# Output gates of a gated linear attention made from a tanh, and two weight splits moved into the state chain

## The reference

```python
def gla_mixer(h, s0, w_in, w_gate, b_gate, norm_w, w_out):
    q, k, v, r, gl = jnp.split(h @ w_in, ...)
    ...
    o, s_new = gla_recurrence(q, k, v, log_a, s0)
    o = rms_norm(o, norm_w) * jax.nn.silu(r.reshape(N, T, H_C, DV_C).astype(jnp.float32))
    return o.reshape(N, T, H_C * DV_C).astype(h.dtype) @ w_out, (s_new,)
```

## Time and profile before

| | |
|---|---|
| median of 3 runs | 1903.7 us (1898.15 to 1910.28) |
| the profiled execution | 1904.86 us, of which its span is 1903.2 |
| PE busy | 1788.3 us (94%) |
| DVE busy | 889.6 us (47%) |
| ACT busy | 465.1 us (24%) |
| POOL busy | 78.5 us (4%) |
| mean granted TensorE clock | 0.94 |

### The profile page before, as it was taken

The page is one execution under the profiler, slowest core; times in us unless marked ns, Lnnn a source line. Parts: engine busy times, 40 slices in busy tenths (PEclk is TensorE's granted clock), DMA queues, the critical chain, the costliest instruction groups (busy, mean ns, idle before and its releaser), DMA issues.

```text
span 1903.2 us, 32761 instructions
## 1 busy us (share of the span) xinstructions
PE 1788.3 (94%) x14212; PEld 1630.2 (86%) x14212; DVE 889.6 (47%) x1650; ACT 465.1 (24%) x746; POOL 78.5 (4%) x146
## 2 busy tenths in 40 slices
PE   5979999999999899999999899878988999999998
PEld 3768888777768899999999897767878999999997
DVE  3534243344344653636353523376565745454442
ACT  1512221134463311111111324122322311111112
POOL 2000001500030000000000000000000000000000
PEclk7889999989999999999999999877779999999998
DMA  9657665410062222222223465122232222222211
GB/s 352 227 196 248 223 199 166 177 51 1 23 223 90 67 79 78 88 88 87 67 88 126 146 199 177 46 70 70 70 120 89 67 89 72 82 88 88 78 54 50
DMA packets 160179, 218.83 MB, mean 115 GB/s; under 512 B 7271, under 2 KB 131198, under 8 KB 159630
## 3 DMA queue, kind: packets, MB, share of 16 engines
q1 hardware_dynamic: 148814, 177.52, 28.4%
q0 software_dynamic: 11264, 39.86, 6.0%
HBM read 199.66 MB, written 21.76 MB: 116 GB/s over the span
## 4 chain that ended last, share of the span: by engine, by line
PE 89%; DVE 7%; ACT 1%; DMA 1%; issue 1%; SPq 0%; ACTq 0%; DVEq 0%
PE ps L1365 14%; PE ps L1363 14%; PE ps L1362 14%; PE ps L1041 4%; PE ps L1042 4%; PE ps L1043 4%; PE ps L918 3%; PE ps L1151 2%; PE ps L1328 2%; PE ps L1329 2%; PE ps L1331 2%; PE ps L1137 2%; PE ps L967 1%; PE ps L1166 1%; PE ps L1459 1%
## 5 line engine op out<-in xcount | busy, mean ns | idle before, releaser
L1362 PE MATMUL ps<-arena_r,wring_r 128*128 128x288 f32 x2048 | 570.1, 293 | 7.4 <-DVE hbuf_r L2131 7.4
L1365 PE MATMUL ps<-arena_r,wring_r 128*128 128x288 f32 x2048 | 439.6, 296 | 0.0
L1362 PEld LDWEIGHTS ps<-arena_r,wring_r 128*128 128x128 f32 x2048 | 386.0, 188 | 7.7 <-issue 7.7
L1365 PEld LDWEIGHTS ps<-arena_r,wring_r 128*128 128x128 f32 x2048 | 328.3, 188 | 0.0
L1363 PE MATMUL ps<-hbuf_r,wring_r 128*128 128x288 f32 x1024 | 286.1, 295 | 0.0
L1363 PE MATMUL ps<-arena_r,wring_r 128*128 128x288 f32 x1024 | 284.6, 294 | 0.0
L1833 ACT ACTIVATE wring_r<-wring 128x2048 fp32r<-128x2048 f32 x64 | 122.5, 1917 | 620.5 <-DMA wring<-in_mlp_w 620.5
L1363 PEld LDWEIGHTS ps<-hbuf_r,wring_r 128*128 128x128 f32 x1024 | 193.9, 189 | 0.0
L1363 PEld LDWEIGHTS ps<-arena_r,wring_r 128*128 128x128 f32 x1024 | 192.4, 188 | 0.0
L2469 DVE SCALAR_TENSOR_TENSOR xbuf<-ps,mod,xbuf 128x288 f32<-128x288 f32 (+1 forms) x128 | 56.1, 480 | 245.5 <-PE ps L1365 245.5
L1041 PE MATMUL ps<-wring_r,xbuf_r 128*128 128x512 f32 x360 | 149.9, 416 | 0.0
(11 more groups left out here) (378 smaller groups left out, 2627.2 us busy)
## 6 DMA issues: line engine op xcount, KB each, us to landing
wring<-in_mlp_w SPq DMA_DIRECT2D x64, 1024.0 KB, 5.2
arena<-in_ada_w SPq DMA_DIRECT2D x40, 1024.0 KB, 5.8
wring<-in_even_w_in SPq DMA_DIRECT2D x14, 1024.0 KB, 8.2
wring<-in_gla_w_in SPq DMA_DIRECT2D x12, 1024.0 KB, 5.6
wring<-in_ada_w SPq DMA_DIRECT2D x4, 2048.0 KB, 28.1
xbuf<-xspill SPq DMA_DIRECT2D x2, 2304.0 KB, 9.3
arena<-in_cache_cmp_kv POOLq DMA_DIRECT2D x16, 256.0 KB, 10.1
wring<-in_cache_diff_k POOLq DMA_DIRECT2D x16, 256.0 KB, 3.6
```

The lines of the kernel that those rows point to most:

```text
L1362: pe.matmul(bank, hi, x_hi[:, k, cols], start=k == 0, stop=False)
L1365: mm = pe.matmul(bank, lo, x_hi[:, k, cols], start=False, stop=k == KC - 1)
```

## The change

Four edits, all in layer 1's recurrence:

- ACT's exponential of -r becomes a tanh of r/2 (one instruction for one, same buffers, same waits).
- A gate becomes one DVE instruction, (tanh + 1) times r, in place of three.
- The factor 1/2 and the norm weight go elsewhere: the two columns of norm weight in `v2T` are halved once, before the recurrence, and `g_gated` multiplies output, halved weight and gate in one scalar_tensor_tensor, where it was a tensor_tensor.
- The low halves of `W_R[2]` and `W_R[3]` are no longer made after the last gate of heads 0 and 1 but inside the chain of heads 1 and 2, after its first two states.

```diff
--- before.py
+++ after.py
@@ -1937,7 +1937,7 @@
                 act.wait_ge(r_kept, i + 1)
                 if i >= 2:
                     act.wait_ge(r_ready, i - 1)
-                act.activation(er[i % 2], gr[:, i // 2, halves[i % 2]], ACT.Exp, scale=-1.0).then_inc(r_exp, 1)
+                act.activation(er[i % 2], gr[:, i // 2, halves[i % 2]], ACT.Tanh, scale=0.5).then_inc(r_exp, 1)
 
             def g_square(h):
 
@@ -2602,6 +2602,8 @@
                     dve.sem_inc(st_kept, 1)
                     if h == 0 and p < 2:
                         rest_unit(W_R[p], S_GIN + 8 + p)
+                    elif 1 <= h <= 2 and p == 0:
+                        rest_unit(W_R[h + 1], S_GIN + 9 + h)
                     if h + 1 < HC:
                         if p == 1:
                             g_offsets(h + 1)
@@ -2624,17 +2626,16 @@
 
                 c, cols = i // 2, halves[i % 2]
                 dve.wait_ge(r_exp, i + 1)
-                step(dve.tensor_scalar(er[i % 2], er[i % 2], 1.0, None, ALU.add))
-                step(dve.reciprocal(er[i % 2], er[i % 2]))
-                dve.scalar_tensor_tensor(out=gr[:, c, cols], in0=gr[:, c, cols], scalar=v2T[:, V2_GLAN + c % 2:V2_GLAN + c % 2 + 1],
-                                         in1=er[i % 2], op0=ALU.mult, op1=ALU.mult).then_inc(r_ready, 1)
+                dve.scalar_tensor_tensor(out=gr[:, c, cols], in0=er[i % 2], scalar=1.0, in1=gr[:, c, cols],
+                                         op0=ALU.add, op1=ALU.mult).then_inc(r_ready, 1)
 
             def g_gated(h):
 
                 dve.wait_ge(r_mm, 2 * KC)
                 dve.wait_ge(go_kept, h + 1)
                 for e in range(2):
-                    ins = dve.tensor_tensor(hT[:, 2 * h + e, :], go[:, e, h, :], gr[:, 2 * h + e, :], ALU.mult)
+                    ins = dve.scalar_tensor_tensor(out=hT[:, 2 * h + e, :], in0=go[:, e, h, :], scalar=v2T[:, V2_GLAN + e:V2_GLAN + e + 1],
+                                                   in1=gr[:, 2 * h + e, :], op0=ALU.mult, op1=ALU.mult)
                 return ins
 
             for u in range(len(gin)):
@@ -2654,6 +2655,7 @@
                 elif u == V_HALF + 2:
                     g_from_blocks(0)
             dve.wait_ge(ada_kept, 2 * ADA)
+            dve.tensor_scalar(v2T[:, V2_GLAN:V2_GLAN + 2], v2T[:, V2_GLAN:V2_GLAN + 2], 0.5, None, ALU.mult)
             step(dve.memset(gatt[:, :, :, :], 0.0))
             g_scores(0)
             g_sample_keys(0)
@@ -2679,8 +2681,6 @@
                     if h + 2 < HC:
                         for i in range(at + 3, last):
                             r_gate(i)
-                    if h < 2:
-                        rest_unit(W_R[h + 2], S_GIN + 10 + h)
             ins = g_gated(HC - 1)
             step(ins)
             head_rates(1)
```

## The result

| | before | changed |
|---|---|---|
| median of 16 runs each | 1905.14 us (1896.19 to 1912.58) | 1889.55 us (1882.84 to 1902.42) |
| ratio of the runs | | 0.9925 (95%: 0.9905 to 0.9944) |
| span of the profiled execution | 1903.2 us | 1881.7 us |
| PE's waits for L2596 | 18.8 us | 2.8 us |
| first L1476 of head 0's samples to first L1328 of the output projection ("the stretch") | 152.63 us | 135.27 us |

The changed kernel is faster by 0.75% (0.56 to 0.95%); 1886.6 us and a ratio of 0.9910 were forecast.

What follows compares the result with a forecast made beforehand. PE was taken to bound the kernel, waiting on DVE for the first state at the seams between heads. Terms 8.9 + 6.85 + 1.4 = 17.1 us took 1903.7 to 1886.6 us, range 1878 to 1893.5.

Steps and rivals of the forecast that it cites:

- What bounds it: Recurrence: PE, 89% of the chain, waits 18.8 us for L2596, one wait per seam, the third 0.3 us.
- First seam: Between heads 0 and 1: three shorter gates and the moved low half let L2596 start 8.9 us sooner.
- Second seam: Between heads 1 and 2: two shorter gates and the moved low half let L2596 start 6.85 us sooner.
- The moved low halves: Behind the first state steps of heads 1 and 2: cost nothing, 2.28 us each under 7.31 us of DVE idle time.
- rival 2: Heads 1 and 2: no cover for the moved low halves, gain only 12.1 us, time 1891.6 us; chance 0.09.
- After the last head: End of head 3: shorter gates free DVE before PE starts, so PE leads; 1.4 us gained.
- Tanh and the halving: ACT's tanh replaces exp one for one without more table loads; halving the norm weight before the recurrence costs nothing.
- rival 3: ACT: tanh and exp lie in two tables, loads cost 7.7 us, gain 9.4, time 1894.3 us; chance 0.02.
- The clock: Both seams: PE's clock rises as long after resumption as now (7.9 and 7.5 us), worth 0 us.
- rival 1: Seams: clock returns sooner, gain 19 to 24.7 us; chance 0.18, 0.03 for the far end, 1879 us.
- rival 4: Heads 1 and 2: the clock, having fallen, does not rise; 37 us slower, 1941 us; chance 0.03.
- The time: Whole kernel: 17.1 us (0.90%) less than 1903.7 gives 1886.6 us.

Runs made afterwards that it cites:

- e3: Changed kernel with 12 extra reciprocals (result unused) on DVE behind each of the two moved low halves; 1883.3 us, one run, stretch 136.2 us.
- e4: Changed kernel with 24 extra reciprocals (result unused) on DVE behind each of the two moved low halves; 1913.2 us, one run, stretch 156.5 us.
- e1: Changed kernel with the two low halves put back after the last gate of heads 0 and 1; median 1890.0 us, ratio 0.9912, stretch 142.2 us.
- e5: Changed kernel with a sigmoid in place of the tanh, which needs five more table loads; 1882.6 us, one run, stretch 136.2 us.
- e6: Changed kernel with the next head's first two states ahead of sample keys and gates, low half behind the gates; median 1889.2 us, ratio 0.9894, stretch 128.8 us.
- e10: The kernel of e6 run again, on the same chip as the changed kernel; median 1885.5 us, ratio 0.9899, stretch 132.6 us.
- e9: Changed kernel unaltered, run again beside the kernel before; median 1889.0 us, ratio 0.9904, stretch 135.32 us.
- e2: Kernel before with only the two low halves moved, old gates kept; median 1902.0 us, ratio 0.9969, stretch 145.6 us.
- e7: Changed kernel with 30 reciprocals (result unused) between sample keys and gates at the first two seams; 1924.6 us, one run, stretch 169.4 us.

## Why the prediction was right

- **What bounds it.** Right: PE's waits for L2596 gave 16.0 of the 17.4 us. 18.8 us became 2.8, "about 3" by the forecast. One reading was wrong and cost nothing: the third wait, 0.33 us, isn't between heads 2 and 3 but ahead of head 0's first outputs (1215.45 before, 1216.75 now). DVE's busy time fell by 35.7 us, where 36 was forecast.
- **First seam, 8.9 us.** Measured 9.09. Gates were a little cheaper than taken (0.45 us each, not the 0.52 of a gate that reads its weight column); the ACT wait of the third tanh is there.
- **Second seam, 6.85 us.** Measured 6.99.
- **The moved low halves, nothing.** Right, with DVE's wait for ACT at 0.49 us where 0.5 was forecast. The size of the cover was wrong: I read it as DVE's idle time less the insertion, 5 us left. It ends only when PE asks for the fifth state (e3, e4), so rival 2 had less behind it than the 0.09 I gave. I also priced the move only by its own length; e1 shows that without it the shortened gates would have run into ACT's rounding, 1.4 us more.
- **After the last head, 1.4 us.** Measured 1.40. The gated product takes 810 ns, the upper bound I took was 814, and PE leads as forecast: DVE now sits idle 2.93 us before the sample states of head 3.
- **Tanh and the halving.** Right: table loads at the same places, tanh 437 to 439 ns as exp. But the price in rival 3, every load on PE's path, was wrong: e5 has five of them at no visible cost. By e5 that rival would not have given 9.4 us of gain but 16 to 17.
- **The clock, 0.** The sum came out right, its steps not quite. The clock came back 7.0 and 6.8 us after PE resumed, not 7.5 to 7.9; that gave 0.7 us. It also fell somewhat earlier against PE's work in heads 1 and 2 and took 0.7 us again. The windows, to set beside the earlier trace rows:

```profile
1257.60:1274.60 17.00, 15.05 (x66) 0.50 0.28 93
1302.00:1319.00 17.00, 15.70 (x69) 0.50 0.28 84
1274.60:1302.00 27.40, 26.90 (x253) 1.00 0.20 63
```

- **Rivals 1 and 4.** Neither came. The clock fell at the samples in every profile, with PE's wait at 0, 1.5 or 20 us, so the far end of rival 1, a slow stretch that goes away with the waits, is out; and it rose again each time, so rival 4 is out. The clock can give some us all the same, 3.8 between e6 and e10, but with the same waits in both: that goes with the execution and not with the change.
- **The time.** 17.1 us of stretch were forecast, 17.4 measured (and 17.3 in e9 against the same profile of before). The medians moved by 15.6, and the interval of the ratio, 0.56 to 0.95%, is 11 to 18 us. That the mechanism holds is shown by the waits; that the stretch agrees to 0.3 us is partly luck. The kernel before was profiled once, and the clock alone has moved the stretch by 2.6 us against the forecast in e2 and by 3.8 us between e6 and e10.

## What to carry to other kernels

Cost a shortened helper engine by the wait it feeds, walk its new order row by row from the trace, and include what the neighbours make for it: a step that becomes early can meet an input that is not ready (ACT's rounding here). Read the cover of an inserted step from when the bounding engine asks for the next thing, not from the helper's idle time. And look for the stretch in which the bounding engine runs at half clock: here it was worth more than the waits that remained, and the way to it was which work stands in that stretch.

## What the hardware showed that I had not expected

- **The clock's return doesn't follow the pause.** Measured from PE's resumption with r products right behind: 7.9 and 7.5 us (pauses 10.6, 7.9), 7.0 and 6.8 (1.5, 0.9), 7.0 and 7.9 in e1 (5.2, 3.1), 6.7 and 5.1 in e2 (8.4, 5.7), 5.1 and 5.4 in e7 (20.7, 20.0), and without any wait 5.2 and 5.3 in e6, 5.5 and 6.5 in e10. Between 5 and 8 us, in no order of the pause. Where the clock falls moves more than its return: in e6 it fell 4.9 us ahead of head 2's first output products, in e10 10.6 us ahead, and half of this, 2.8 us, is most of the 3.8 us between their stretches.
- **Full clock, two rates.** The MLPs are the same list of PE work in every kernel, at a granted clock of 1.00, without waits. From first to last L1365 the first MLP took 404.6 to 405.4 us in twelve of the thirteen profiles and 400.9 in one (e6). The second took about 405 in seven and 400.1 in six. (The 394.9 us that the expectation for e9 names is wrong: it counts e7's second MLP only up to 1890 us; whole it is 405.1.) The windows show the rate, here 40 us in the second MLP of the kernel before and of the changed one:

```profile
1600.00:1640.00 40.00, 40.00 (x306) 1.00 0.23 79
```

```profile
1584.00:1624.00 40.00, 40.00 (x310) 1.00 0.24 79
```

306 or 310 products in 40 us. It goes with the execution, not with the kernel (the changed kernel had 400.1 in one profile and 405.1 in the next). It explains 5 of the 21.5 us between the two profiled spans; its cause stays open, and no run here was made for it.
